# The router's logits with the tokens as the standing operand, and tile 0's share ahead of tile 1's transposes

## The reference, cut to what matters

```python
h = rmsnorm(x, pre_ffn_g[l])
# moe_ffn
t = h.reshape(-1, D)                                   # 256 x 1024
logits = t.astype(jnp.float32) @ router_w              # 256 x 8
vals, idx = lax.top_k(logits, TOP_K)                   # best two experts of each token
probs = jax.nn.softmax(vals, axis=-1)
gates = jnp.sum(jax.nn.one_hot(idx, N_EXPERTS) * probs[..., None], axis=1)
for e in range(N_EXPERTS):
    y = y + gates[:, e:e + 1] * swiglu(t, wg[e], wu[e], wd[e])
```

## Time and profile before

| | |
|---|---|
| median of 3 runs | 1450.05 us (1449.87 to 1450.07) |
| the profiled execution | 1450.18 us |
| its span, first to last instruction | 1448.3 us |
| PE busy | 1430.4 us (99% of the span) |
| DVE busy | 1194.2 us (82%) |
| ACT busy | 1030.7 us (71%) |
| share of PE in the chain that ended last | 94% |
| granted TensorE clock, mean | 0.999 |

### The profile page before, as it was taken

How to read it: one execution, slowest core, us unless ns; L and a number is a source line. 1 busy time by engine, 2 the same in 40 slices (tenths; PEclk the granted TensorE clock), 3 DMA queues, 4 the chain that set the end, 5 groups by cost and what they waited for, 6 DMA issues and landing times.

```text
span 1448.3 us, 20771 instructions
## 1 busy us (share of the span) xinstructions
PE 1430.4 (99%) x7088; PEld 1190.6 (82%) x7088; DVE 1194.2 (82%) x1376; ACT 1030.7 (71%) x1256; POOL 14.5 (1%) x13
## 2 busy tenths in 40 slices
PE   9999999999999999999999999999999999999997
PEld 7988888887987688888888888888888888888885
DVE  7777565556876799899898989989889989889997
ACT  6765454455575677887787787787778778777774
POOL 0000000000000200000000000000000000001000
PEclk9999999999999999999999999999999999999999
DMA  9435965544524499999999999999999999999991
GB/s 375 175 131 209 369 238 201 204 174 175 182 110 160 151 422 400 354 392 398 367 388 395 372 365 402 366 368 401 386 352 399 391 377 364 397 381 366 420 397 67
DMA packets 68899, 454.11 MB, mean 314 GB/s; under 512 B 9456, under 2 KB 9712, under 8 KB 17008
## 3 DMA queue, kind: packets, MB, share of 16 engines
q1 hardware_dynamic: 61056, 432.47, 77.0%
q10 hardware_dynamic: 6640, 16.78, 3.2%
q0 software_dynamic: 1152, 4.19, 0.7%
HBM read 438.21 MB, written 15.20 MB: 313 GB/s over the span
## 4 chain that ended last, share of the span: by engine, by line
PE 94%; DVE 3%; ACT 2%; issue 1%; DVEq 0%
PE psum L480 26%; PE psum L482 26%; PE psum L481 26%; PE psum L827 7%; PE psum L830 3%; PE psum L889 2%; PE psum L487 1%; ACT lru_b L1007 1%; DVE hn L1395 0%; PE psum L651 0%; PE psum L592 0%; DVE xs L1401 0%; PE psum L872 0%; PE psum L507 0%; DVE hn L1379 0%
## 5 line engine op out<-in xcount | busy, mean ns | idle before, releaser
L1290 DVE TENSOR_TENSOR w_lo<-ring,w_hi 128x1024 fp32r<-128x1024 f32 x812 | 940.8, 1219 | 51.9 <-ACT w_hi L994 51.1
L994 ACT ACTIVATE w_hi<-ring 128x1024 fp32r<-128x1024 f32 x812 | 807.3, 1052 | 54.4 <-PE psum L482 48.9
L480 PE MATMUL psum<-w_hi,hT_both 128*128 128x512 f32 (+1 forms) x1120 | 434.3, 388 | 2.0 <-DVE hT_both L1301 2.0
L482 PE MATMUL psum<-w_hi,hT_both 128*128 128x512 f32 (+1 forms) x1120 | 426.7, 381 | 0.0
L481 PE MATMUL psum<-w_lo,hT_both 128*128 128x512 f32 (+1 forms) x1120 | 425.9, 380 | 0.0
L480 PEld LDWEIGHTS psum<-w_hi,hT_both 128*128 128x128 f32 x1120 | 210.7, 188 | 43.5 <-DVE hT_both L1301 4.5
L482 PEld LDWEIGHTS psum<-w_hi,hT_both 128*128 128x128 f32 x1120 | 210.6, 188 | 41.1
L481 PEld LDWEIGHTS psum<-w_lo,hT_both 128*128 128x128 f32 x1120 | 211.0, 188 | 38.4 <-issue 0.4
L480 PE MATMUL psum<-w_hi,act_hi 128*128 128x512 f32 x560 | 218.8, 391 | 0.8 <-DVE act_lo L1301 0.8
L482 PE MATMUL psum<-w_hi,act_lo 128*128 128x512 f32 x560 | 218.2, 390 | 0.0
L481 PE MATMUL psum<-w_lo,act_hi 128*128 128x512 f32 x560 | 218.2, 390 | 0.0
(11 more groups left out here) (239 smaller groups left out, 880.2 us busy)
## 6 DMA issues: line engine op xcount, KB each, us to landing
ring<-moe_gate SPq DMA_DIRECT2D x112, 1024.0 KB, 7.2
ring<-moe_up SPq DMA_DIRECT2D x112, 1024.0 KB, 7.5
ring<-moe_down SPq DMA_DIRECT2D x112, 1024.0 KB, 7.5
ring<-in_units SPq DMA_DIRECT2D x19, 1024.0 KB, 7.3
ring<-dense_gate SPq DMA_DIRECT2D x14, 1024.0 KB, 4.9
ring<-dense_up SPq DMA_DIRECT2D x14, 1024.0 KB, 4.8
ring<-dense_down SPq DMA_DIRECT2D x14, 1024.0 KB, 4.9
ring<-out_units SPq DMA_DIRECT2D x8, 1024.0 KB, 7.8
```

Of the source, the lines that this page charges most:

```text
L480: pe.matmul(dst, s_hi, m_hi, start=start, stop=False)
L482: return pe.matmul(dst, s_lo, m_hi, start=False, stop=stop)
L994: act.activation(w_hi[:, h % AHEAD, :], ring[:, n % RING, (h % 2) * HCOLS:(h % 2 + 1) * HCOLS], ACT.Copy).then_inc(hi_ready, 1)
L1290: dve.tensor_tensor(w_lo[:, h % AHEAD, :], ring[:, (h // 2) % RING, (h % 2) * HCOLS:(h % 2 + 1) * HCOLS], w_hi[:, h % AHEAD, :].bitcast(F3 ...
```

## The change

The router's products have their operands exchanged: a tile's 128 tokens of `hT` stand, the router's 8 columns move, and the logits come out as 128 x 8 in bank 5, where DVE reads them. The copy by DVE, the two small transposes and the two semaphores between them go. The products are made per tile and half in a new function `route`; tile 0's stand between the warm-ups and tile 1's transposes, with three warm-ups there in place of four, and `norm_transposes`, which had no other caller, goes. There are 48 of these products in place of 24.

```diff
-        logitsT = flat(lru_g)[:, 0:T]
...
-        logitsT_ready = sem("logitsT_ready")
-        logitsT_copied = sem("logitsT_copied")
...
-            def norm_transposes(layer, which):
-
-                n = 2 * layer + (which == PRE_FFN)
-                norm_head(n)
-                warm(4, 7)
-                turn_rows_of(n, 1)
-                warm(1, 7)
...
-            norm_transposes(1, PRE_FFN)
-            for k in range(DK):
-                if k % 4 == 0:
-                    norm_wait(1, PRE_FFN, k // 4)
-                mm = product(ps[4][0:EXPERTS, 0:T], (rw_hi[:, k, :], rw_lo[:, k, :]), hT(k),
-                             start=(k == 0), stop=(k == DK - 1))
-            mm.then_inc(logitsT_ready, 1)
-            pe.wait_ge(logitsT_copied, 1)
-            for tt in range(TT):
-                mm = pe.transpose(ps[5][:, tt * EXPERTS:(tt + 1) * EXPERTS],
-                                  logitsT[0:EXPERTS, tt * P:(tt + 1) * P], ident[0:EXPERTS, 0:EXPERTS])
-            mm.then_inc(logits_ready, 1)
+            def route(tt, half):
+
+                norm_wait(1, PRE_FFN, half, tt)
+                for k in range(4 * half, 4 * half + 4):
+                    mm = product(ps[5][:, tt * EXPERTS:(tt + 1) * EXPERTS], hT(k, tt * P, (tt + 1) * P),
+                                 (rw_hi[:, k, :], rw_lo[:, k, :]), start=(k == 0), stop=(k == DK - 1))
+                return mm
+
+            norm_head(2 * LAYERS - 1)
+            warm(3, 7)
+            route(0, 0)
+            route(0, 1)
+            turn_rows_of(2 * LAYERS - 1, 1)
+            warm(1, 7)
+            route(1, 0)
+            route(1, 1).then_inc(logits_ready, 1)
             warm(2, 6)
             pe.wait_ge(mask_ready, 1)
...
-            dve.wait_ge(logitsT_ready, 1)
-            dve.tensor_copy(logitsT[0:EXPERTS, :], ps[4][0:EXPERTS, 0:T]).then_inc(logitsT_copied, 1)
             dve.wait_ge(logits_ready, 1)
```

## The result

| | median | all runs |
|---|---|---|
| kernel before | 1450.03 us | 1449.87 to 1450.15, 12 runs |
| changed kernel | 1453.36 us | 1450.49 to 1453.67, 12 runs |
| forecast | 1449.8 us | range 1448.2 to 1452.3 |

The ratio after to before is 1.0017, with a 95% interval of 1.0009 to 1.0024. Not only the median moved. The kernel before scatters by 0.3 us, the changed one by 3.2: of its twelve runs seven lie between 1453.29 and 1453.67, two at 1451.8 and 1451.9, three between 1450.49 and 1450.64. Where the clock fell in the eleven runs without a profile, no record shows. The time lies outside the forecast's range, and the way is the rival's that was given 16%: the clock.

The account below looks back on a forecast made before the run. PE bounds the kernel, busy 99% of the span. Copy and turning back gone (-0.78), tile 1's products shorter (-0.24) and its transposes late (+0.71) gave about -0.3 us: 1449.8 us, range 1448.2 to 1452.3.

Parts of the forecast that it names:

- the rival's that was given 16%: Router stretch, 472 to 489 us: thin products stream almost nothing, TensorE's clock falls, time taken as 1455 us; chance 0.16.
- The schedule: Router stretch: tile 0's loads from 471.93, tile 1's transposes about 474.6, its first load 476.7, logits at DVE about 479.5.
- The pace of the thin products: Router products with 128 standing, 8 moving columns: weight loads set 0.11 us each, so 24 take 2.81 us.
- The rival of quicker loads: Router products: fp32r loads go at 0.074 us each, nothing is late, median 1448.2 us; chance 0.08.
- the gain carries to the end: From 489 us on PE has no idle time, so its earlier gain or loss reaches the end undiminished.
- the full clock behind the 0.11 of tile 1's 24 products: Tile 1's router products: 0.11 us each assumes TensorE at 2.4 GHz, giving 2.81 us instead of 3.05.
- The sum (-0.78 - 0.24 + 0.71): Logits at DVE: copy and turning back gone, tile 1's products shorter, its transposes late; together about -0.3 us.
- L632's sixteen thin products: Argument against a clock fall: products of 128 standing, 8 moving columns, sixteen in 1.74 us, left the clock full.
- one of its two cases: Clock falls but returns before the gather: products 2.5 us and mask products 0.6 us more, 1452.9 us.
- The single value that the prediction took for the rival: Clock fall in the router stretch: 1455 us, taken with cases of 1452.9 and 1457.5; chance 0.16.
- a clock that stays low through the gather: Clock not back before the gather: gather adds 3.7 us and a warm-up 0.9, giving 1457.5 us.
- Everything decides at one point: Test named in advance: whether PE's granted clock leaves 1.00 between 472 and 489 us.

Follow-up runs that it names:

- e1: The changed kernel with the router's 8 moving columns repeated 16 times (128 columns) in every router product; 1449.94 us median, runs 1449.90 to 1450.04.
- e4: The kernel before with products per tile and half, tile 0's ahead of tile 1's transposes, three warm-ups; router columns still stand, copy and turning back stay; 1448.69 us.
- e8: e4 with tile 0's logits copied and turned back early and the warm-up behind tile 1's transposes left out; 1448.52 us.
- e2: The changed kernel with tile 0's products moved behind tile 1's transposes and four warm-ups in front of these; 1454.88 us, runs 1452.39 to 1457.21.
- e7: e2 with 128 moving columns instead of 8 in all 48 products; 1451.69 us, runs 1451.58 to 1451.80.
- e5: The changed kernel with 128 moving columns in tile 0's 24 products only; 1450.00 us, five of eleven runs 1450.58 to 1452.29.
- e6: The changed kernel with 128 moving columns in tile 1's 24 products only; 1449.99 us, five of eleven runs 1451.18 to 1455.19.
- e12: e7 with three warm-ups instead of four before tile 1's transposes, PE idle 2.0 us there; 1451.72 us, four of eleven runs 1453.16 to 1456.95.
- e11: e7 with two warm-ups instead of four before tile 1's transposes, PE idle 2.8 us there; 1453.17 us, seven of eleven runs 1453.13 to 1458.39.
- e3: The changed kernel with the fourth warm-up put back in front of tile 0's products; 1452.85 us, eight of eleven runs 1451.23 to 1454.09.

## Why the prediction was wrong

- **The schedule was right.** At a full clock, in e1, tile 1's first product starts at 476.7, the logits reach DVE at 479.65 (forecast 479.5), and the kernel takes 0.17 us less than before (forecast 0.3; the interval, 0.999 to 1.0008, can't tell this from nothing, but the trace has the same 0.18). In the changed kernel itself tile 0's 24 loads start at 471.88 (forecast 471.93), 0.11 apart, and tile 1's eight transposes follow without a wait between the halves.
- **The pace of the thin products was right:** 0.11, from L632, the mask products and the 192 ns loads. The rival of quicker loads (1448.2) is out: the changed kernel's loads in fp32r took 186 to 192 ns at a full clock, against 192 ns of the fp32 loads of the earlier trace rows. The rule of the Trainium skill (TensorE: Matmul & The Clock Gate, Weight-path perf modes) would have made it about half; these loads don't agree with it.
- **That the gain carries to the end was right**, for gain and loss alike (e1, e4, e8, and the 3.34 us of the loss).
- **The step that failed is the full clock behind the 0.11 of tile 1's 24 products.** The sum (-0.78 - 0.24 + 0.71) has no term for the clock. The prediction put its fall at 16%, on the argument that "L632's sixteen thin products, twice in the kernel, left the clock full", though, as it said itself, those stood amid dense products. Here 24 thin products stand where a warm-up and idle time were, eight transposes and one warm-up follow, and then 24 more. In the profiled execution the clock fell to 0.50 before tile 1's products, which then stood 0.213 us apart; the time was 1453.36 us instead of 1449.8. e1, e2 and e7 show that the thin streaming is the cause, e5 and e6 that either half of it is enough in some runs. e12 shows that an empty place in the warm-up's stead can lose the clock as well.
- **The rival had the right mechanism and, in one of its two cases, nearly the right price.** If the clock is back before the gather it gave 1452.9: 2.5 us on the products, 0.6 on the mask products. Measured 1453.36, with 2.4 on the products, 0.7 on the first of them behind a slow warm-up, which was left out, and 0.58 at the mask, though through the two warm-ups that PE was still in and not through the mask products. That the sum still came close is in part luck: one term was missing and one stood for another cost. The single value that the prediction took for the rival was 1455, about halfway between 1452.9 and the 1457.5 of a clock that stays low through the gather. That longer fall did not come in the changed kernel. In e2 the clock came back within the gather, and its slowest run (1457.21) is 5.5 us above the 1451.69 of its own order at a full clock (e7).
- **"Everything decides at one point" was right as a test, but the answer isn't one for all runs.** The same kernel gave 1450.5 and 1453.7. A forecast of such a case needs the scatter as a part of it; mine had the clock as a matter of yes or no.

## What to carry to other kernels

Which operand stands is a question of what each instruction streams. With few columns on one side, let the few stand: 0.06 us a product against 0.11 here, and the engine keeps streaming. Where the many must stand, the load's time is paid anyway, so fill it with columns: repeating the 8 columns 16 times cost no time here and saved 3.4 us, which brings the change back to the time before and not below it. Read PE by its columns and the granted clock, never by its busy share; and where a change thins the work near a wait, time it in many runs, since one profile can catch a good one: those of e5, e6, e11 and e12 all did. A move and an exchange in one edit are better tried apart: the move was worth -1.4 us, the exchange took 1.2 of it back and lost the clock besides.

## What the runs showed of the hardware

- At the lower clock level weight loads slow down with the matmuls: the 128-column loads took 333 ns instead of 192 and stood 0.213 us apart instead of 0.11, in this row of the changed kernel (min/median/max over both levels):

```profile
L477 PEld LDWEIGHTS psum<-rw_hi,hT_both x16: 186/240/333, 471.9 to 481.7; 128*128 128x128 f32 x16
```

- Warm-ups can hold PE up once the clock has fallen: the two behind the products took 3.36 us there, and PE came to the mask products 0.9 us after the mask. Whether they brought the clock back sooner, no run shows.
- In the profiled execution of the change the clock fell with PE busy without a gap from 472.0 to 475.2; by the times it fell in every run of the change. It came back at 485.5, at the end of the two warm-ups. In e2 it was low from 478.5 to 492.0, in e3 from 481.0 to 487.8.
- On the transposes between the two thin stretches the Trainium skill (TensorE: Matmul & The Clock Gate, Part 4) says that they don't count as PE-busy the same way. No run here sets them apart.
